# FFN gate/up: two of every four contraction tiles as seven block products, with their sums on VectorE

## The reference

```python
def swiglu_ffn(x, w_gate_up, w_down):
    gate, up = jnp.split(x @ w_gate_up, 2, axis=-1)
    return (jax.nn.silu(gate) * up) @ w_down
```

## Time and profile before

| | |
|---|---|
| median of 3 runs | 2954.94 us (2952.25 to 2955.64) |
| the profiled execution's own time | 2950.0 us |
| its span, first to last instruction | 2948.2 us |
| mean granted TensorE clock | 0.986 |
| TensorE busy | 96% of the span, 13696 matmuls |
| VectorE busy | 61%, 2183 instructions |
| ScalarE busy | 51%, 1978 instructions |
| HBM read | 489.86 MB, 167 GB/s over the span |
| first loop of groups (FFN of layer 0) | about 1031 to 1694 us of the span |
| second loop of groups (FFN of layer 1) | about 2225 to 2888 us of the span |

### The profile page before, as it was taken

How to read it: one execution, slowest core, us unless ns; L and a number is a source line. 1 busy time by engine, 2 the same in 40 slices (tenths; PEclk the granted TensorE clock), 3 DMA queues, 4 the chain that set the end, 5 groups by cost and what they waited for, 6 DMA issues and landing times.

```text
span 2948.2 us, 39238 instructions
## 1 busy us (share of the span) xinstructions
PE 2823.6 (96%) x13696; PEld 2342.0 (79%) x13696; DVE 1800.2 (61%) x2183; ACT 1497.7 (51%) x1978; POOL 30.2 (1%) x29
## 2 busy tenths in 40 slices
PE   7989999999988999999999999799989999999997
PEld 6778887887866788888888878688878888888886
DVE  5767877877876555555555554556664555555555
ACT  6676767677664444444444444454444444444443
POOL 0000000000000000000000000000000000000000
PEclk9999999999998999999999999899999999999999
DMA  6434444444433555555555555533336555565553
GB/s 239 153 122 150 154 157 147 162 138 159 159 114 97 168 185 193 192 190 190 190 185 190 193 176 190 174 119 111 107 126 209 185 188 193 188 195 190 191 192 129
DMA packets 135079, 493.02 MB, mean 167 GB/s; under 512 B 15008, under 2 KB 15328, under 8 KB 134624
## 3 DMA queue, kind: packets, MB, share of 16 engines
q1 hardware_dynamic: 133776, 487.82, 50.1%
q10 hardware_dynamic: 1232, 4.23, 0.4%
HBM read 489.86 MB, written 2.13 MB: 167 GB/s over the span
## 4 chain that ended last, share of the span: by engine, by line
issue 56%; PE 40%; DVE 1%; DMA 1%; ACT 1%; POOL 0%; POOLq 0%; ACTq 0%; SPq 0%; DVEq 0%
PE ACC L527 12%; PE ACC L529 12%; PE ACC L528 12%; PE SIDE L535 1%; DMA RAW<-stream 1%; DVE W_LO L1258 1%; PE SIDE L854 0%; PE SIDE L828 0%; ACT W_HI L909 0%; PE SIDE L851 0%; PE SIDE L833 0%; PE SIDE L838 0%; PE SIDE L866 0%; DVE H L1283 0%; ACT WORK L914 0%
## 5 line engine op out<-in xcount | busy, mean ns | idle before, releaser
L1258 DVE TENSOR_TENSOR W_LO<-RAW,W_HI 128x1024 fp32r<-128x1024 f32 x912 | 1100.5, 1222 | 767.9 <-ACT W_HI L909 764.2
L909 ACT ACTIVATE W_HI<-RAW 128x1024 fp32r<-128x1024 f32 x912 | 959.7, 1059 | 1008.0 <-PE ACC L529 983.4
L527 PE MATMUL ACC<-W_HI,X_HI 128*128 128x512 f32 x2496 | 990.2, 397 | 16.9 <-DVE W_LO L1258 12.5
L528 PE MATMUL ACC<-W_LO,X_HI 128*128 128x512 f32 x2496 | 975.7, 391 | 0.0
L529 PE MATMUL ACC<-W_HI,X_LO 128*128 128x512 f32 x2496 | 975.5, 391 | 0.0
L527 PEld LDWEIGHTS ACC<-W_HI,X_HI 128*128 128x128 f32 x2496 | 471.2, 189 | 112.1 <-issue 18.0
L529 PEld LDWEIGHTS ACC<-W_HI,X_LO 128*128 128x128 f32 x2496 | 470.7, 189 | 99.7
L528 PEld LDWEIGHTS ACC<-W_LO,X_HI 128*128 128x128 f32 x2496 | 471.4, 189 | 93.0 <-issue 0.5
L527 PE MATMUL ACC<-W_HI,A_HI 128*128 128x512 f32 x1024 | 410.2, 401 | 13.1 <-issue 10.4
L529 PE MATMUL ACC<-W_HI,A_LO 128*128 128x512 f32 x1024 | 403.0, 394 | 0.0
L528 PE MATMUL ACC<-W_LO,A_HI 128*128 128x512 f32 x1024 | 402.3, 393 | 0.0
(11 more groups left out here) (247 smaller groups left out, 1688.8 us busy)
## 6 DMA issues: line engine op xcount, KB each, us to landing
RAW<-stream SPq DMA_DIRECT2D x912, 512.0 KB, 3.9
WORK<-gdn_rows ACTq DMA_DIRECT2D x8, 512.0 KB, 4.2
WORK<-xt SPq DMA_DIRECT2D x4, 512.0 KB, 9.3
H<-x SPq DMA_DIRECT2D x2, 1024.0 KB, 13.3
out<-WORK SPq DMA_DIRECT2D x4, 512.0 KB, 3.9
WORK<-tails SPq DMA_DIRECT2D x2, 512.0 KB, 11.1
WORK<-gfin SPq DMA_DIRECT2D x1, 1024.0 KB, 8.3
K<-consts SPq DMA_DIRECT2D x1, 518.0 KB, 6.7
```

Of the source, the lines that this page charges most:

```text
L527: nc.tensor.matmul(dst, hi[:, at:at + P], wh, start=first and h % 2 == 0 and q == 0, stop=False)
L528: nc.tensor.matmul(dst, hi[:, at:at + P], wl, start=False, stop=False)
L909: nc.scalar.activation(W_HI[:, h % WS, :], raw_piece(h), ACT.Copy).then_inc(hi_ready, 1)
L1258: nc.vector.tensor_tensor(W_LO[:, h % WS, :], raw_piece(h), W_HI[:, h % WS, :].bitcast(f32), SUB).then_inc(lo_ready, 1)
```

## The change

In the loop passes (groups 1 to 10 of each FFN; group 0 and the last pass keep their products) the 16 contraction tiles of gate/up are taken as four quartets j = 0 to 3. Tiles 4j+2 and 4j+3 are multiplied as before. Tiles 4j and 4j+1 are done in Strassen's scheme in Winograd's form. The two token tiles, the two contraction tiles and two halves of the 1024 columns (each half has 256 gate and 256 up columns) make 2x2 blocks; seven block products stand in place of eight, each still three matmuls. The four results c11 to c22 gather in SIDE[1] and SIDE[0], the four products that belong to more than one result (m1, m6, m7, m5) in ACC[0] and ACC[1], over all four j.

Each j has six slots of `W_HI`/`W_LO` in place of four: "11" (2 block products, 6 matmuls), "21" (1, a slot filled by half), "13" (2), "24" (2), "pa" (4) and "pb" (4): 15 block products, 45 matmuls, where there were 16 and 48. The slots "13" and "24" hold sums of weight blocks, `t13` and `t24`, formed by VectorE in SBUF before ScalarE and VectorE split them. The weights in HBM are permuted, and the number of pieces is as before.

For the sums on the activation side VectorE forms, once for each FFN during group 0, `x_sum` (high plus low, 2048 columns) and four differences of 512 columns (`token_sums`); ScalarE and VectorE split these into `Z_HI`, `Z_LO`.

After the 24 slots of a pass ScalarE copies m1 out of ACC[0], VectorE forms `dif` and three more sums of 512 columns (`c_add`), then adds `c_add` to SIDE in two instructions of 1024 columns (`c_sum`). The silu and the product with up now read `c_sum` in SBUF and come while the down stripes run; the transposes of `hid` stand before the last down stripe. ScalarE takes them to a buffer `hid_t` in SBUF, from which `A_HI` is made when the down stripes are done, and `A_LO` at slot 20 of the next pass.

SyncE's loop in the FFN has 24 loads in its body in place of 4. The slots of `RAW` are freed in the order of `RAW_FREE`: the first piece of a quartet by the low part of "11", the second by that of "21", the others by "pa" and "pb". The semaphore values of all later stages are shifted; their work is the same. Pass 10 of each loop is unrolled.

```diff
+FFN_PIECE = {"11": 0, "21": 1, "13": 0, "24": 0, "pa": 2, "pb": 3}
+FFN_ORDER = 4 * ["11 21 13 24 pa pb"]
+FFN_OPS = [(kind, j, 4 * j + FFN_PIECE[kind]) for j in range(4) for kind in FFN_ORDER[j].split()] +     [("d", n, 16 + n) for n in range(8)]
+FFN_AT = {op[:2]: e for e, op in enumerate(FFN_OPS)}
+RAW_FREE = [FFN_AT[kind, j] for j in range(4) for kind in ("11", "21", "pa", "pb")] + [24 + n for n in range(8)]
...
+        t13, t24, c_add, dif, c_sum = w(4096, 1024), w(5120, 1024), w(8192, 2048), w(7168, 512), w(10240, 2048)
+        hid_t, z_sum, x_sum = w(12288, 1024), w(6144, 2048), w(10240, 2048)
+        Z_HI, Z_LO = (TR, UR), (NR, YQ)
...
+        def up_products(pe, c, e):
+            kind, j, _ = FFN_OPS[e]
+            pe.wait_ge(lo_ready, c + (e + 1))
+            m1, m6, m7, m5 = (ACC[i][:, k * COLS:(k + 1) * COLS] for i in range(2) for k in range(2))
+            c11, c12, c21, c22 = (SIDE[1 - i][:, k * COLS:(k + 1) * COLS] for i in range(2) for k in range(2))
+            kt = 4 * j + (2 if kind[0] == "p" else 0)
+            a11, a21, a12, a22 = (tuple(b[:, at:at + P] for b in (X_HI, X_LO))
+                                  for at in ((kt + q) * SEQ + t * P for q in range(2) for t in range(NT)))
+            z5, z7, z6, z3 = (tuple(b[i][:, k * COLS + j * P:k * COLS + (j + 1) * P] for b in (Z_HI, Z_LO))
+                              for i in range(2) for k in range(2))
+            f, l = j == 0, j == 3
+            early = f and FFN_AT["pa", 0] < FFN_AT["24", 0]
+            todo = {"11": [(m1, a11, 0, f, l), (c12, z3, 1, f, False)],
+                    "21": [(c11, a12, 0, f, False)],
+                    "13": [(m5, z5, 0, f, l), (m7, z7, 1, f, l)],
+                    "24": [(m6, z6, 0, f, l), (c21, a22, 1, f and not early, False)],
+                    "pa": [(c11, a11, 0, False, False), (c21, a21, 0, early, False), (c12, a12, 1, False, False),
+                           (c22, a22, 1, f, False)],
+                    "pb": [(c12, a11, 0, False, l), (c22, a21, 0, False, l), (c11, a12, 1, False, l),
+                           (c21, a22, 1, False, l)]}[kind]
+            for dst, (hi, lo), half, start, stop in todo:
+                wh, wl = (b[:, e % WS, half * COLS:(half + 1) * COLS] for b in (W_HI, W_LO))
+                m = three(dst, hi, lo, wh, wl, start, stop)
+            m.then_inc(w_used, 1)
...
+            for e in range(0 if first or final_ else 24):
+                if e == 0:
+                    pe.wait_ge(acc_out[0], ph.before("m16", it))
+                if e == FFN_AT["24", 0] or FFN_OPS[e][0] == "pa" and e < FFN_AT["24", 0]:
+                    pe.wait_ge(side_out[0], ph.before("hid_t", it))
+                if e == FFN_AT["13", 0]:
+                    pe.wait_ge(acc_out[1], ph.before("m57", it))
+                up_products(pe, c, e)
+            for k in range(0 if first else 4):
+                pe.wait_ge(acc_out[k % 2], ph.before(f"down{k}", it))
+                if k == 0:
+                    pe.wait_ge(act_lo, it + (FBLK if ph is FFN1 else 0))
+                if k == 3 and not final_:
+                    pe.wait_ge(hid_done, it + (FBLK - 1 if ph is FFN1 else 0))
+                    turn(by_block(hid), 0)
+                for half in range(2):
+                    products(pe, c, 24 + 2 * k + half, k % 2, A_HI, A_LO, True, True)
+                if final_ and nxt and k:
+                    norm_tensor(pe, nxt, k - 1, ((k - 1) % 2, ph.after(f"down{k - 1}", it)))
...
+            for e in range(0 if first or final_ else 24):
+                if e == 20:
+                    act.wait_ge(w_used, c + 19)
+                    nc.scalar.activation(c_add[:, 0:COLS], ACC[0][:, 0:COLS], ACT.Copy).then_inc(m1_out, 1)
+                ffn_hi(act, ph, base, ob, it, e + WS)
...
+            for k in range(0 if first else 4):
+                if k == 1 and not final_:
+                    for t in range(NT):
+                        act.wait_ge(c_out[t], it + late)
+                        gate_out(act, c_sum[:, t * 1024:(t + 1) * 1024], t)
+                if k == 3 and not final_:
+                    take_out(act, 0, ph.after("hid_t", it), hid_t)
...
+                act.wait_ge(w_used, c + (16 if first else 32))
+                act.wait_ge(side_out[0], ph.after("hid_t", it))
+                nc.scalar.activation(A_HI[:, :], hid_t, ACT.Copy).then_inc(act_hi, 1)
...
+        def ffn_lo(dve, ph, base, ob, it, e):
+            (kind, j, piece), wrap = ffn_ahead(it, e)
+            dve.wait_ge(hi_ready, ffn_c(ob, it) + (e + 1))
+            hi, lo = W_HI[:, e % WS, :].bitcast(f32), W_LO[:, e % WS, :]
+            if kind == "21":
+                nc.vector.tensor_tensor(lo[:, 0:COLS], raw_piece(piece)[:, COLS:2 * COLS], hi[:, 0:COLS],
+                                        SUB).then_inc(lo_ready, 1)
+            else:
+                src = {"13": t13, "24": t24}.get(kind, raw_piece(piece))
+                nc.vector.tensor_tensor(lo, src, hi, SUB).then_inc(lo_ready, 1)
+            for n in range(3):
+                weight_sum(dve, ph, base, ob, it, e + 2 - n, n)
+        def weight_sum(dve, ph, base, ob, it, e, n):
+            (kind, j, piece), wrap = ffn_ahead(it, e)
+            if kind != "11":
+                return
+            b11_22, b12_21 = raw_piece(piece), raw_piece(piece + 1)
+            done = sums_done(ph, it, wrap) + 3 * j
+            if n < 2:
+                dve.wait_ge(lo_ready, ffn_c(ob, it) + (e - 3 + n))
+            if n == 0:
+                for p in (piece, piece + 1):
+                    dve.wait_ge(raw_full[p % RAWS], (ffn_raw(base, it) + 24 * wrap) * (16 // RAWS) + 16 * (p // RAWS + 1))
+                i = nc.vector.tensor_tensor(tiles2(t13), tiles2(b11_22),
+                                            b12_21[:, 0:COLS].unsqueeze(1).broadcast_to([P, 2, COLS]), ADD)
+            else:
+                dve.wait_ge(t_done, done + n)
+                a = (t13 if n == 1 else t24)[:, 0:COLS]
+                b = (b11_22 if n == 1 else b12_21)[:, COLS:2 * COLS]
+                i = nc.vector.tensor_tensor(t24[:, (n - 1) * COLS:n * COLS], a, b, ADD)
+            i.then_inc(t_done, 1)
...
+            def hid_lo():
+                dve.wait_ge(act_hi, it + hi0)
+                nc.vector.tensor_tensor(A_LO[:, :], hid_t, A_HI[:, :].bitcast(f32), SUB).then_inc(act_lo, 1)
...
+            for e in range(0 if first or final_ else 24):
+                if e == 20:
+                    hid_lo()
+                if e == 22:
+                    dve.wait_ge(w_used, c + 22)
+                    dve.wait_ge(m1_out, it + late)
+                    nc.vector.tensor_tensor(dif, ACC[0][:, COLS:2 * COLS], c_add[:, 0:COLS], SUB).then_inc(acc_out[0], 1)
+                ffn_lo(dve, ph, base, ob, it, e + WS)
+                if e == 22:
+                    m7, m5 = ACC[1][:, 0:COLS], ACC[1][:, COLS:2 * COLS]
+                    dve.wait_ge(acc_out[0], ph.after("m16", it))
+                    nc.vector.tensor_tensor(c_add[:, 1024:1024 + COLS], m7, dif, SUB).then_inc(mix, 1)
+                    nc.vector.tensor_tensor(c_add[:, COLS:1024], m5, dif, ADD)
+                    dve.wait_ge(mix, it + late)
+                    nc.vector.tensor_tensor(c_add[:, 1024 + COLS:2048], m5, c_add[:, 1024:1024 + COLS],
+                                            SUB).then_inc(acc_out[1], 1)
+            for k in range(0 if first else 4):
+                if k == 0 and not final_:
+                    dve.wait_ge(acc_out[1], ph.after("m57", it))
+                    dve.wait_ge(w_used, c + 24)
+                    for t in range(NT):
+                        at = slice(t * 1024, (t + 1) * 1024)
+                        nc.vector.tensor_tensor(c_sum[:, at], SIDE[1 - t][:, :], c_add[:, at], ADD).then_inc(c_out[t], 1)
+                if k == 1 and not final_:
+                    for t in range(NT):
+                        up = c_sum[:, t * 1024:(t + 1) * 1024].rearrange("p (h two n) -> p h two n", h=2, two=2)[:, :, 1, :]
+                        to, by = (b[:, t * COLS:(t + 1) * COLS].rearrange("p (h n) -> p h n", h=2) for b in (hid, sg))
+                        dve.wait_ge(silu_f, 2 * it + (2 * late + t - 1))
+                        i = nc.vector.scalar_tensor_tensor(to, up, rstd_c[:, t:t + 1], by, MUL, MUL)
+                    i.then_inc(hid_done, 1)
+                for half in range(2):
+                    e = 24 + 2 * k + half
+                    if half == 1:
+                        add_to_h(dve, c + (26 + 2 * k), k % 2, k)
+                    if final_:
+                        split_lo(dve, c, e + WS)
+                    else:
+                        ffn_lo(dve, ph, base, ob, it, e + WS)
...
+            def feed_ffn(base, ob):
+                def next_piece(it, p):
+                    sp.wait_ge(lo_ready, ffn_c(ob, it) + (RAW_FREE[p - RAWS] + 1 if p >= RAWS else p - RAWS + 1))
+                    load_piece(it * 12 + (base - 4 + p // 2), p)
```

(27 more changed lines are left out.)

292 lines of the change are left out of this document (187 added, 105 removed).

## The result

The changed kernel takes 2933.5 us (median of 5 runs, 2930.4 to 2936.56), the kernel before in the same comparison 2952.42 us (5 runs). The ratio is 0.9935, with a 95% interval of 0.992 to 0.995: faster by 19 us, where the prediction said 48. So it is faster, at less than half of the forecast gain; the time lies within the stated range (2895 to 2940), far from the forecast case.

What follows compares the result with a forecast made beforehand. TensorE alone was taken to bound the loops. 2950.0 - 54.4 (matmuls) + 6 (loads) + 0.8 (group 0) - 0.6 (last pass) = 2901.8 against the profiled execution, 2906.7 us for the median; range 2895 to 2940.

Steps and rivals of the forecast that it cites:

- the forecast case: Whole kernel: 2906.7 us, bounds 2896.7 (no stall, clock kept) to 2917 (stall of 0.85 a pass); chance 0.64.
- What bounds the kernel, and what is removed: Loop passes: TensorE alone sets the time; 12 of 288 matmuls go, 66.19 to 63.47 us a pass, -54.4 us.
- The spacing kept at 0.2267: TensorE in the loop passes: the new matmuls, of the same shape, still start 0.2267 us apart.
- The semaphore increments: Slot ends on TensorE: eight more cost nothing by the trace row; rival by the skill's rule, 4.2 us, 2911, chance 0.03.
- VectorE's prices: VectorE in a loop pass: its instructions sum to 55.4 or 61.0 us of 63.47, so they fit.
- The walk: Order within a pass: each operand is ready in time, thinnest slack 0.4 us at "pa"; the new wait is for loads.
- L up to 5.1 us costs nothing: Weight sums of quartets 2 and 3: load landing time L is free to 5.1 us, then costs 2(L - 5.1) a pass.
- the rival that ends slower: Weight sum in `RAW`, quartets 2 and 3: loads stall passes in full, 2969 us at L = 6.8; chance 0.08.
- The ring of loads: Load into `RAW` and VectorE's work that frees its slot: L + 5.46 us against 10.20; taken as 0.3 a pass, +6 us.
- the ring binds in part: Rival, loads into `RAW`: L of 5.5 to 6.2 gives 0.8 to 2.2 a pass, 2917 to 2945 us; chance 0.13.
- Group 0: Group 0 of each FFN: making the token sums and `Z_HI`, `Z_LO` delays TensorE, +0.4 us for each FFN (0 to 1).
- The last pass: End of each FFN: TensorE's idle time falls from 3.89 to about 3.6 us, -0.3 each, with the clock fall left in.

Runs made afterwards that it cites:

- the variants without either fault: Changed kernel with the first weight sum one position later, plus Z buffers right behind X (2897.97 us) or X read in place of the token sums (2899.56 us).
- the variant with both faults mended: Changed kernel with each quartet's first weight sum one position later on VectorE and the Z buffers right behind X in SBUF: 2897.97 us, ratio 0.9817.
- Z near X: Z buffers moved in SBUF to right behind X: 2933.15 us on the changed kernel alone, 2897.97 us on the one with the first weight sum later.
- the sum one position earlier: Changed kernel with each quartet's first weight sum one position earlier in VectorE's order: 3072.33 us, ratio 1.0408.

## Why the prediction was wrong

- *What bounds the kernel, and what is removed:* right. Twelve matmuls at 0.2267 us fewer make a pass of 63.47; the variants without either fault take 63.49 us. The forecast of 2906.7 was even above what the scheme gives when nothing stalls, 2895.7 to 2898.6.
- *The spacing kept at 0.2267:* wrong in the slots of 84 of the 276 matmuls, by some 5 ns on the mean. "The new matmuls have the same shape" was true, but 48 of them read a new operand, whose place in SBUF I had not looked at. It was priced among the rivals ("1% on 0.2267 would be 0.6 a pass, 12 us"), with the wrong reason; alone it is worth 0.4 a pass. In the changed kernel it is hidden behind the ring.
- *The semaphore increments:* the row was right. The Trainium skill ("TensorE: Matmul & The Clock Gate", The cost: per-tile semaphore tail) has increments on completion serialise, 26 ns each. No trace here shows it: with 32 slots a pass of 63.49 us is 276 x 0.2267 and 0.92, with 24 it was 288 x 0.2267 and 0.90, where the rule would add 0.21.
- *VectorE's prices:* right. The additions of 512 columns, of which before had no row, in the loops of the first FFN (xcount, busy us, mean ns):

```profile
L1659 DVE TENSOR_TENSOR WORK<-WORK,RAW 128x512 f32<-128x512 f32 x72 | 49.2, 683 | 0.0
...
L1653 DVE TENSOR_TENSOR WORK<-RAW 128x1024 f32<-128x1024 f32 x35 | 42.8, 1224 | 44.2 <-DMA RAW<-stream 44.2
```

  0.683 us alone against "near 0.69", and 56.3 us busy in a pass between the ends 55.4 and 61.0. VectorE at 88% isn't a bound by itself: the same work fits into 63.49.
- *The walk:* right in its order and in its first place, "pb" of the third quartet (1197.90 above). It left out a second: it never walked the first sum of the next pass, which stands in front of an add to `H` and delays the transposes by 0.3 and 0.4 us a pass. The loads there land after 4.5 us on the mean, which "L up to 5.1 us costs nothing" had as free. The text had such a stall only under the rival that ends slower.
- *The ring of loads:* the step that failed. The walk gave L up to 5.1 us as free and 2(L - 5.1) above it, and I took 0.3 us a pass, from the middle of the earlier trace rows (4.6, 5.2, 5.9): 6 us in the sum. By the table the passes take 14.4 + 19.6 = 34 us more than in the variant with both faults mended, 1.7 a pass. At its own place the formula held: the ring's loads at 5.4 and 5.6 us on the mean of each FFN give 0.6 and 0.9, and 0.7 and 0.9 is what TensorE loses ahead of "pb". So the term was too small by half a microsecond a pass there, because L was. The rest is the place that wasn't walked (0.3 to 0.4) and the spacing (0.4), which the sum had at nothing; without the spacing the ring takes its share too (2933.15 with Z near X). The rival "the ring binds in part" (2917 to 2945), which had 0.13, names the cause; that its middle of 2930 lies so near 2933.5 is in part luck, since at the place it speaks of the loss is at the low end of its 0.8 to 2.2 a pass.
- *Why L was higher:* L was a constant taken from the second load of a pair, and here the ring's load goes out as the fourth in 5.4 us (at 1173.7, 1176.0, 1177.8 and 1179.1; they land after 3.8, 4.6, 4.8 and 5.2). That alone would by the formula have cost 0 to 0.4 a pass: in the variant with both faults mended the same loads land after 5.1 to 5.3 us on the mean. But a late sum bunches the lows behind it, which bunches the next loads: 5.3 to 5.7 in the changed kernel, 5.7 to 5.9 with the sum one position earlier. A load's time answers to the schedule.
- *Group 0:* +1.2 and +1.3 us against +0.4 (0 to 1), above its own bounds; no run looks for the reason. *The last pass:* the stall is 3.63 us, as forecast (3.6), and the clock falls behind it as before, from the second row on:

```profile
1692.96 0.77 PE L563 MATMUL ACC<-W_HI,A_HI 128*128 128x512 f32 x1 [3.63 <-issue]
1693.53 0.63 PE L564 MATMUL ACC<-W_LO,A_HI 128*128 128x512 f32 x1
1693.95 0.63 PE L565 MATMUL ACC<-W_HI,A_LO 128*128 128x512 f32 x1
```

- *The sum again:* 2950.0 - 54.4 + 34 + 2.5 - 0.6 = 2931.5, and 4.6 us that the profiled execution is later before the first FFN, make 2936.1 for its 2936.56. The match is partly luck: by the table the passes of the mended variant, the last stalls with them, are 52.8 shorter than before and not 55.0, and the two stretches behind the FFNs are 0.8 and 0.9 shorter.

What stays open: which matmul is late, and why. Averaged over 36 quartets of the first FFN, the three starts of "21", which reads X alone, are followed by the next after 0.228, 0.233 and 0.235 us, though X lies well; the last three of "24", also X, by 0.231, 0.227 and 0.227; with Z near X all are 0.2267. So a matmul between others that read Z is late too. Nor was another difference than 128 bytes tried, or what part of the two operands' reading collides.

## What to carry to other kernels

When a change takes work from the engine that bounds and fills another that works in order, look for the wait on that engine whose release goes round through a load's buffer, and write the ring out, at every place of the pass where it waits, the wrap to the next pass too. Price the load by the bunch in which it will go out, not by a row of a quiet stretch: here one sum moved by one position was worth 30 us to the good and 139 to the bad. And when a new tensor becomes a matmul's operand, compare the addresses of both operands; a table allocated in between can shift them apart.

## What the runs showed of the hardware that I had not expected

- Matmuls of 512 columns (fp32r, 128 by 128 stationary) start 0.2267 us apart when the stationary and the moving operand have the same place within 512 bytes of a partition, both at 128 (2897.97 us) or both at 0 (2895.7 us), and 0.2325 to 0.233 apart on the mean when they differ by 128 bytes, whichever of the two lies on the multiple (2917.25 us with Z and A there, by its down stripes; 2942.62 us with the weights there). The last three times are of one run each, and 256 bytes in place of 512 would fit as well.
- Loads of 512 KB issued 1 to 2 us apart land after 3.8, 4.6, 4.8, 5.2 us in one bunch and 4.1, 5.4, 6.8, 6.9 us in a tighter one, at a mean DMA share of 0.53 to 0.61; with half the bytes the longest is 3.8 and 4.0 in two runs. The mean share doesn't tell the bunches apart.
